# A Griffin-style hybrid decoder trunk: the first modulation in blocks of 128 output features

## What is computed

```python
mod = jax.nn.silu(c) @ w_ada + b_ada
sh1, sc1, gt1, sh2, sc2, gt2 = [m[:, None, :] for m in jnp.split(mod, N_MOD, axis=-1)]
h = _rmsnorm(x, g_pre_mix) * (1.0 + sc1) + sh1
proj = h @ w_in
(qa, ka, va, qb, kb, vb, qi, ki, wi, ga, gb) = jnp.split(proj, cuts, axis=-1)
...
y_a = _moba_attention(qa, ka, va)
y_b = _dsa_attention(qb, kb, vb, qi, ki, wi)
mixed = jax.nn.sigmoid(ga) * y_a + jax.nn.sigmoid(gb) * y_b
x = x + gt1 * _rmsnorm(mixed @ w_out, g_post_mix)
h = _rmsnorm(x, g_pre_ffn) * (1.0 + sc2) + sh2
f = (jax.nn.silu(h @ w_gate) * (h @ w_up)) @ w_down
return x + gt2 * _rmsnorm(f, g_post_ffn)
```

## Time and profile before

| | us |
|---|---|
| median of 3 runs | 891.45 (891.27 to 893.38) |
| the profiled execution | 891.98 |
| its span | 890.1 |
| TensorE busy in the span | 867.8 (97%) |
| VectorE busy | 660.2 (74%) |
| ScalarE busy | 411.6 (46%) |
| GpSimd busy | 133.0 (15%) |

### The profile page before, as it was taken

The page is one execution under the profiler, slowest core; times in us unless marked ns, Lnnn a source line. Parts: engine busy times, 40 slices in busy tenths (PEclk is TensorE's granted clock), DMA queues, the critical chain, the costliest instruction groups (busy, mean ns, idle before and its releaser), DMA issues.

```text
span 890.1 us, 11600 instructions
## 1 busy us (share of the span) xinstructions
PE 867.8 (97%) x4241; PEld 713.6 (80%) x4241; DVE 660.2 (74%) x1090; ACT 411.6 (46%) x607; POOL 133.0 (15%) x164
## 2 busy tenths in 40 slices
PE   7999999999999999999999999999999999999996
PEld 5787788888877788888878778888888788888885
DVE  3778999887878767667568899988787865654842
ACT  1264654655636354344336555555564534434421
POOL 6500300200312030110232030020031200000302
PEclk9999999999999999999999999999999999999998
DMA  9787665567442977676634756566744274564611
GB/s 333 298 300 299 214 243 207 216 237 256 143 166 72 361 276 292 246 289 251 235 142 146 292 223 237 214 236 237 244 158 166 73 302 170 219 260 182 209 52 47
DMA packets 35577, 194.61 MB, mean 219 GB/s; under 512 B 4544, under 2 KB 4544, under 8 KB 19008
## 3 DMA queue, kind: packets, MB, share of 16 engines
q1 hardware_dynamic: 33984, 189.62, 57.8%
q0 software_dynamic: 1536, 4.24, 1.5%
HBM read 192.80 MB, written 1.05 MB: 218 GB/s over the span
## 4 chain that ended last, share of the span: by engine, by line
PE 80%; issue 9%; DVE 8%; DMA 2%; POOL 1%; ACT 1%; SPq 0%; DVEq 0%; POOLq 0%; ACTq 0%
PE ps L1142 23%; PE ps L1144 23%; PE ps L1143 23%; PE ps L1196 4%; PE ps L1248 1%; PE ps L1296 1%; DMA raw<-w_ada 1%; DVE pj L983 1%; DVE ffn_m L848 1%; PE ps L1276 1%; DVE x L1006 1%; DVE pj L968 1%; PE ps L1269 1%; PE ps L1268 1%; PE ps L1247 1%
## 5 line engine op out<-in xcount | busy, mean ns | idle before, releaser
L803 DVE TENSOR_TENSOR w_lo<-raw,w_hi 128x2048 fp32r<-128x2048 f32 (+1 forms) x132 | 302.2, 2298 | 52.2 <-ACT w_hi L581 50.3
L1142 PE MATMUL ps<-w_hi,t_hi 128*128 128x512 f32 (+2 forms) x832 | 325.3, 391 | 2.3 <-DVE t_lo L951 1.6
L1144 PE MATMUL ps<-w_hi,t_lo 128*128 128x512 f32 (+2 forms) x832 | 318.7, 383 | 0.0
L1143 PE MATMUL ps<-w_lo,t_hi 128*128 128x512 f32 (+2 forms) x832 | 318.1, 382 | 0.0
L581 ACT ACTIVATE w_hi<-raw 128x2048 fp32r<-128x2048 f32 (+1 forms) x132 | 249.8, 1896 | 25.4 <-DMA raw<-w_stream 16.0
L1142 PEld LDWEIGHTS ps<-w_hi,t_hi 128*128 128x128 f32 x832 | 156.3, 188 | 35.1 <-DVE t_lo L951 3.1
L1144 PEld LDWEIGHTS ps<-w_hi,t_lo 128*128 128x128 f32 x832 | 156.3, 188 | 30.9
L1143 PEld LDWEIGHTS ps<-w_lo,t_hi 128*128 128x128 f32 x832 | 156.5, 188 | 28.6
L1142 PE MATMUL ps<-w_hi,m_hi 128*128 128x512 f32 x240 | 99.6, 415 | 0.3
L1144 PE MATMUL ps<-w_hi,m_lo 128*128 128x512 f32 x240 | 94.3, 393 | 0.0
L1143 PE MATMUL ps<-w_lo,m_hi 128*128 128x512 f32 x240 | 93.7, 390 | 0.0
(11 more groups left out here) (170 smaller groups left out, 898.6 us busy)
## 6 DMA issues: line engine op xcount, KB each, us to landing
raw<-w_stream SPq DMA_DIRECT2D x128, 1024.0 KB, 5.9
ada<-w_ada SPq DMA_DIRECT2D x84, 512.0 KB, 5.0
raw<-w_ada SPq DMA_DIRECT2D x6, 512.0 KB, 11.8
raw<-w_stream SPq DMA_DIRECT2D x4, 656.0 KB, 8.6
scale_t<-gains POOLq DMA_DIRECT2D x4, 512.0 KB, 4.4
gate_t<-gains POOLq DMA_DIRECT2D x4, 512.0 KB, 5.1
pj<-w_ada SPq DMA_DIRECT2D x3, 512.0 KB, 16.1
mixed<-w_ada SPq DMA_DIRECT2D x2, 512.0 KB, 12.5
```

Of the source, the lines that this page charges most:

```text
L803: nc.vector.tensor_tensor(w_lo[:, U % RING, 0:n], raw[:, U % RAW, 0:n], w_hi[:, U % RING, 0:n].bitcast(F32), ALU.subtract).then_inc(s_lo, 1)
L1142: nc.tensor.matmul(dst, hi, w_h, start=first, stop=False)
L1143: nc.tensor.matmul(dst, hi, w_l, start=False, stop=False)
L1144: return nc.tensor.matmul(dst, lo, w_h, start=False, stop=last)
```

## The change

The host lays the scale and shift part of the first layer's `w_ada` out anew: eight blocks (`ada_first`), one for each 128 output features, each 128 x 2,048 (1 MB): the scale's half with the input features on the partitions, the shift's half with the output features there. x is normed without scale and shift. For each block `k` (`first_block`, `first_h`, `first_hi`, `first_lo`):

- TensorE sums the scale of 128 features into one column (eight matmuls of one column) and turns the 128 features of normed x, both into one bank;
- VectorE multiplies the shift's 128 x 1,024 numbers with c, which lies along the rows of all partitions (`c_rows`), and sums them in the same instruction; it then scales and shifts the turned x with one instruction over 256 columns, as scale and shift are now one number per partition;
- ScalarE rounds it, VectorE makes the remainder;
- TensorE multiplies this block of features with its rows of chunks 0, 1 and 2 (`first_products`). The sums of three chunks and two halves stay open in six banks until the last block.

Chunk 0's units become 0 and 3, chunk 1's unit 1, chunk 2's units 2 and 4. The blocks go through three places (`FIRST_RING`). The units 0 to 4 are split inside the phase. After it TensorE goes on with chunk 3 at once and the turn of the index queries comes behind its first half. The first two pieces of the next table move from before step 2 to its end, behind the two that are there, and SP loads them at the start of step 3. The four tables `scale_t`, `shift_t`, `gate_t`, `acc` become parts of one buffer `wide_t`. Layer 1 is as before.

```diff
+FIRST_RING = 3
+FIRST_ORDER = ((0, False), (0, True), (1, False), (1, True), (2, False), (2, True), (3, False), (3, True),
+               (4, False), (4, True), (5, False), (6, False), (7, False))
...
+    return ([0, 3], [1], [2, 4])[c] if l == 0 else ([0, 1], [2], [3, 4])[c]
...
-START_FILL = (5, 5, 18, 11, 0, 8, 0, 4)
+FIRST_FILL = (16, 10, 10, 8)
...
+        first_at = (mixed[:, :, :].rearrange("p t n -> p (t n)"),
+                    wide_t[:, 0:2, :].rearrange("p t n -> p (t n)"), wide_t[:, 2:4, :].rearrange("p t n -> p (t n)"))
...
+            for i, is_unit in FIRST_ORDER:
+                if is_unit:
+                    load_unit(0, i)
+                    continue
+                if i >= FIRST_RING:
+                    sp.wait_ge(s_mod, i - FIRST_RING + 1)
+                    sp.wait_ge(s_first_sh, i - FIRST_RING + 1)
+                sp.dma_start(first_at[i % FIRST_RING], ada_first[i, :, :]).then_inc(s_first[i % FIRST_RING], 16)
             for l in range(DEPTH):
-                for u in range(RAW, RING):
-                    load_unit(l, u)
-                load_pieces(sum(MIX_PIECES[1]))
...
+                    if s == 3 and l == 0:
+                        load_pieces(sum(MIX_PIECES[1]))
...
+            def first_hi(k):
+                act.wait_ge(s_first_h, k + 1)
+                nc.scalar.activation(t_hi[:, k, :], ffn_m[:, k % 2, :], ACT.Copy).then_inc(s_first_hi, 1)
...
+            act.wait_ge(s_c_wide, 1)
+            nc.scalar.activation(c_rows, ps[:, PTB:PTB + 2, :].rearrange("p b n -> p (b n)"), ACT.Copy).then_inc(s_c_rows, 1)
+            border(-1, False)
+            for k in range(KT):
+                if k in (0, 2, 3, 4, 5):
+                    split_hi(0, (0, 2, 3, 4, 5).index(k))
+                first_hi(k)
...
+            def first_h(k):
+                block = first_at[k % FIRST_RING]
+                dve.wait_ge(s_first[k % FIRST_RING], 16 * (k // FIRST_RING + 1))
+                if k:
+                    dve.wait_ge(s_first_sh, k)
+                nc.vector.tensor_tensor_reduce(junk, block[:, D:], c_rows, 1.0, 0.0, ALU.mult, ALU.add,
+                                               first_shift[:, 0, k:k + 1]).then_inc(s_first_sh, 1)
+                dve.wait_ge(s_mod, k + 1)
+                bank = PTB + k % 2
+                nc.vector.tensor_scalar(first_scale[:, k:k + 1], ps[:, bank, SEQ:SEQ + 1], cols[:, 1, k:k + 1],
+                                        cols[:, 0, k:k + 1], ALU.add, ALU.mult)
+                dve.wait_ge(s_first_sh, k + 1)
+                link(nc.vector.tensor_tensor(first_shift[:, 1, k:k + 1], first_shift[:, 0, k:k + 1], cols[:, 2, k:k + 1],
+                                             ALU.add))
+                nc.vector.tensor_scalar(ffn_m[:, k % 2, :], ps[:, bank, 0:SEQ], first_scale[:, k:k + 1],
+                                        first_shift[:, 1, k:k + 1], ALU.mult, ALU.add).then_inc(s_first_h, 1)
+            def first_lo(k):
+                dve.wait_ge(s_first_hi, k + 1)
+                nc.vector.tensor_tensor(t_lo[:, k, :], ffn_m[:, k % 2, :], t_hi[:, k, :].bitcast(F32),
+                                        ALU.subtract).then_inc(s_first_lo, 1)
...
+            dve.wait_ge(s_c_rows, 1)
+            for k in range(KT):
+                first_h(k)
+                if k == 0:
+                    split_lo(0, 0)
+                first_lo(k)
+                if k in (1, 2, 3, 4):
+                    split_lo(0, k)
+            split_lo(0, RING)
...
+                    if s == 2 and l == 0:
+                        add_pieces(sum(MIX_PIECES[1]))
...
+            def first_block(k):
+                block, bank = first_at[k % FIRST_RING], PTB + k % 2
+                pe.wait_ge(s_first[k % FIRST_RING], 16 * (k // FIRST_RING + 1))
+                if k > 1:
+                    pe.wait_ge(s_first_h, k - 1)
+                elif k == 0:
+                    pe.wait_ge(s_c_rows, 1)
+                for i in range(KT):
+                    nc.tensor.matmul(ps[:, bank, SEQ:SEQ + 1], block[:, i * P:(i + 1) * P], cs[:, i:i + 1],
+                                     start=i == 0, stop=i == KT - 1)
+                if k == 0:
+                    pe.wait_ge(s_xn, TT)
+                turn(ps[:, bank, :], [hbuf[:, t, k * P:(k + 1) * P] for t in range(TT)], s_mod)
...
+            def first_products(ks, chunks):
+                for k in ks:
+                    for these in ((0, 1), (2,)):
+                        for t in range(TT):
+                            for c in these:
+                                if c in chunks:
+                                    first_product(c, t, k)
+            def first_phase():
+                spread_c()
+                fill(2, ones[:, :], ones[:, :], P, FIRST_FILL[0])
+                first_block(0)
+                fill(5, ones[:, :], ones[:, :], P, FIRST_FILL[1])
+                first_block(1)
+                first_products((0,), (0,))
+                fill(5, ones[:, :], ones[:, :], P, FIRST_FILL[2])
+                first_block(2)
+                first_products((1,), (0,))
+                first_products((0, 1), (1,))
+                fill(5, ones[:, :], ones[:, :], P, FIRST_FILL[3])
+                first_block(3)
+                first_products((2,), (0, 1))
+                first_products((0, 1, 2), (2,))
+                first_block(4)
+                first_products((3,), (0, 1, 2))
+                first_block(5)
+                first_products((4,), (0, 1, 2))
+                first_block(6)
+                first_products((5,), (0, 1, 2))
+                first_block(7)
+                first_products((6, 7), (0, 1, 2))
...
+                    project(l, 3, 0)
+                    turn_index(l)
+                    project(l, 3, 1, lambda: index_logits(l, 0))
+                    turn_qk(l, 2)
+                    index_logits(l, 1)
+                for s in range(2 if l else 4, N_CHUNK + 2):
+                    if l == 0 and s == 4:
+                        project(l, s, 0, lambda: index_logits(l, 2))
```

More of the change, by code:

```diff
@@ L362, in wait_multiplied @@
             l, u = U // UNITS, U % UNITS
[L363 to L364 removed]
+            if u in used_units[l]:
+                eng.wait_ge(s_used, l * N_USED + used_units[l].index(u) + 1)
             elif u < OUT_UNIT:
[L366 removed]
+                c = [chunk_units(l, c)[-1] for c in range(N_CHUNK)].index(u)
+                eng.wait_ge(s_mm, l * N_MM + mm_no(c, 1))
             elif u == FFN_UNIT - 1:
@@ L525, in _ @@
             nc.gpsimd.tensor_scalar(quarter, quarter, PI_IN, -PI_IN, ALU.min, ALU.max).then_inc(s_ang, 1)
-            for t in range(TT):
-                norm(t)
             pool.wait_ge(s_sin, 1)
@@ L1071, in _ @@
                         gate_head(l, s - 3, 0)
-                    for u in SPLITS[s][:-1]:
+                    for u in SPLITS[s][1 if s == 2 and l == 0 else 0:-1]:
                         split_lo(l, u)
```

275 lines of the change are left out of this document (128 added, 147 removed).

## The result

| | before | after |
|---|---|---|
| median of 4 runs, us | 891.56 (891.27 to 893.38) | 905.65 (905.02 to 907.83) |
| span of the profiled execution | 890.1 | 903.2 |
| R, end of rope 4 on VectorE | 102.88 | 114.81 |
| span less R | 787.2 | 788.4 |

A forecast was written before the change was run, and what follows sets the result against it. VectorE's chain up to R was taken as the bound, TensorE's 12 us gain being used up in waits; R moves from 102.9 to 107.05, +4.15 us on 891.98 gives 896.1, less 0.5 for the median: 895.7, range 889 to 902.5.

The forecast's parts named there:

- Start of the first phase: From the spread of c (ready at 5.1) through turns, copies, norm and scaling of x: first block's sum starts at 15.0.
- One block on VectorE: Per block 2.85 us, 6.5 with a large weight unit, 5.1 with the small; last block's h ready at 51.1.
- TensorE in that phase: Blocks' products run close behind VectorE, 3.0 us a block; three chunks done at some 56.4, 12 us earlier than before.
- From there to X: From the last h at 51.1 through units 5 to 7, two ropes and the second piece, to 71.15.
- X: Point on VectorE where modulation piece 1, the second piece, is added; forecast at 71.15 us.
- From X to R: Pieces, unit 8's load, ropes 2 to 4 and index sums on VectorE: 35.9 us, so R = 107.05.
- Behind R nothing is changed: After the end of rope 4 the kernel runs as before, so R's shift of +4.15 us is the whole change.
- half clock: Rival: TensorE's clock is down at 31.8, first long burst takes 8.2 us instead of 4.1; 900; 0.22 together with late transfers.
- more waits: Rival: 1 MB transfers in the blocked phase come late, 1 us a block from block 3: +5, 901; 0.22 shared.
- No change: Rival: VectorE's sum over 1,024 takes 0.65 us instead of 1.2; R at 102.7, time 891.3; chance 0.17.
- Faster: Rival: VectorE skips waits for weight rounding in blocks 1 to 4, cheaper handovers; last h 41.5, -5.5, 886; chance 0.13.

The follow-up runs named there:

- runs with one column: Changed kernel with 7 of 8 one-column matmuls left out per block: 900.22 us; also weights rounded ahead: 895.43; instead pieces 1 to 3 before unit 7's split: 892.66.
- gap-filled run: Changed kernel with ten 512-column matmuls into a free bank during TensorE's wait for unit 6 in chunk 3's first half: 904.23 us.

## Why the prediction was wrong

The direction was right, with a chance of 0.67, and so was the frame: R + 787. The size was not: 4.15 us forecast, 13.1 in the span. R came at 114.8 instead of 107.05. Along the prediction's own steps:

- **Start of the first phase**, 15.0: 15.79, 0.8 late. The spread of c is eight matmuls, but 16 instructions, and took 3.8 us (4.38 to 8.15) where the prediction has 1.8: it took the price of one instruction for that of a matmul, as in the step below. An earlier start, shorter copies and shorter scaling gave part of that back.
- **One block on VectorE.** The sum of 1,024 takes 1.22 (1.2 taken), the remainder .42, the waits for rounding 4.9 us in all. (The 5.6 of the prediction does not come out of its own terms, which give 3 x 1.45 + 0.8 = 5.15; the 51.1 uses the terms.) The scaling takes .54, not .42: 1.0 over eight blocks.
- **TensorE in that phase** is the step that failed: "The 64 matmuls of one column, costed at 0.11 each as weight-bound, lie beside VectorE's work." Each is two instructions, .23 together, 1.84 a block; and they lie in front of the turn for which VectorE waits. Their 14.7 us made TensorE the bound: a cycle of 4.97 us (38.88 to 43.85, and the two after it alike), where VectorE's own is 2.9 in blocks 5 to 7. The price is only half of the error: by the prediction's own figures, 0.88 + 3.0 on TensorE against 2.85 on VectorE, TensorE's cycle is the longer one there, and the two were never set side by side. TensorE's cycle cost VectorE 4.3 us of waits and hid the rounding. With the 0.8 and the scaling the last h was ready at 56.85 instead of 51.1. The runs with one column show 5.4 us for it alone.
- **From there to X**: 21.9 us against 20.05 predicted. Of the 1.85 more, 1.65 are the half clock of chunk 3 after its 2.37 us wait (4.4 for 2.75), which the gap-filled run takes away.
- **From X to R**: 36.1 us against 35.9. Piece 3 added at X + 5.2, the unit behind it landed at X + 6.45, TensorE's waits before the turns, the stall beside the all-reduce (109.60, 4.28): all as written. Here the mechanism and the size were right, though TensorE ran at the lower clock once more after the wait for rope 2 (0.50 from 85.1 to 90). What I had not seen is how much of it was to be had back by moving pieces into VectorE's wait (7.8 us).
- **"Behind R nothing is changed"**: 1.2 more. The turn and the first half of chunk 5 take 7.9 us (114.87 to 122.80) for 6.3 before (102.94 to 109.24), with TensorE's clock down after the 2.42 us wait.

0.8 + 4.95 + 1.85 + 0.2 + 1.2 are the 9.0 us between the forecast span (894.2) and the measured one. Of the rivals, *half clock* happened, at four other places than the one it was set at (from 15.9, 67.1, 85.2 and 114.9 us), and *more waits* did, but not from late transfers; the waits were for TensorE. *No change* needed 0.65 us for a sum of 1,024, and the trace has 1.22. *Faster* fell on the same step as the forecast: it too took VectorE's chain for the bound. The transfers of the phase (297 GB/s) held nothing up.

## What to carry to other kernels

When work is cut into blocks that pass through two engines in turn, sum up both engines' cycle per block, every instruction counted, before choosing one as the bound; small matmuls ahead of a handover count in full, and their number of instructions is to be read from a row. Where an experiment that takes a wait away gains nothing, look at what took its place: here 4.9 us of one wait became 6.1 of another. A transfer that may only be issued when older data has been used should not stand, in its own engine's queue, ahead of a load whose buffer is already free, and the work that frees its buffer belongs into a wait, not behind it.
